# State-space decays: the diagonal blocks get their mask on TensorE, the other blocks go from PSUM straight into their final place

## The reference

```python
def chunked_decay_scan(q, k, v, log_a, s0):
    # S_t = a_t S_{t-1} + k_t^T v_t,  y_t = q_t S_t
    cum = jnp.cumsum(log_a ...)
    decay = jnp.exp(jnp.where(lower, cum[..., :, None] - cum[..., None, :], -jnp.inf))
    scores = jnp.einsum('bhnid,bhnjd->bhnij', qc, kc) * decay
    y_intra = jnp.einsum('bhnij,bhnjv->bhniv', scores, vc)
    ...

def bidir_prefix_scan(ctx_in, lat_in):
    yc_f, sc_f = chunked_decay_scan(context, forward, from zero)
    yc_b, sc_b = chunked_decay_scan(flipped context, backward, from zero)
    yl_f, _ = chunked_decay_scan(latent, forward, from sc_f)
    yl_b, _ = chunked_decay_scan(flipped latent, backward, from sc_b)
```

## Time and profile before

| what | value |
|---|---|
| time of three executions, median (lowest to highest) | 1506.96 us (1502.47 to 1507.47) |
| span of the profiled execution, first to last instruction | 1503.5 us (its time around the span isn't given) |
| mean granted clock of PE | 0.971 of 2.4 GHz |
| PE, DVE, ACT, POOL busy | 1422.7, 818.4, 666.7, 835.4 us |
| first `spread` to start of `out1` | 640.16 to 702.66 us |

### The profile page before, as it was taken

The page is one execution under the profiler, slowest core; times in us unless marked ns, Lnnn a source line. Parts: engine busy times, 40 slices in busy tenths (PEclk is TensorE's granted clock), DMA queues, the critical chain, the costliest instruction groups (busy, mean ns, idle before and its releaser), DMA issues.

```text
span 1503.5 us, 22602 instructions
## 1 busy us (share of the span) xinstructions
PE 1422.7 (95%) x8800; PEld 1215.9 (81%) x8800; DVE 818.4 (54%) x1554; ACT 666.7 (44%) x1076; POOL 835.4 (56%) x665
## 2 busy tenths in 40 slices
PE   6989999999999999877999999999999999999997
PEld 3868888999988887544778888888878865999997
DVE  3787677786676697677675333321126667322211
ACT  3436764445452233674442322232226376544442
POOL 0533417998965443664435454554446630699985
PEclk9999999999999999977999999999999999999999
DMA  9656605777775642000445555543333320355563
GB/s 368 258 181 254 231 18 208 254 251 245 241 254 201 216 161 96 15 29 1 143 151 195 196 185 195 187 140 90 103 104 108 112 89 1 114 195 185 182 188 119
DMA packets 71322, 242.98 MB, mean 162 GB/s; under 512 B 7472, under 2 KB 13104, under 8 KB 70832
## 3 DMA queue, kind: packets, MB, share of 16 engines
q1 hardware_dynamic: 68800, 237.15, 46.5%
q10 hardware_dynamic: 2416, 4.39, 1.0%
HBM read 239.42 MB, written 1.05 MB: 160 GB/s over the span
## 4 chain that ended last, share of the span: by engine, by line
PE 51%; DVE 3%; ACT 2%; POOL 1%; issue 1%; DMA 0%; DVEq 0%; ACTq 0%
PE bank L539 15%; PE bank L540 14%; PE bank L541 14%; PE cond_a L960 1%; PE bank L960 1%; PE bank L676 1%; PE cond_a L1020 1%; PE bank L677 1%; PE bank L968 1%; PE bank L680 1%; PE bank L980 1%; PE cond_b L980 0%; PE cond_b L968 0%; ACT w_hi L1278 0%; DVE scratch L2572 0%
## 5 line engine op out<-in xcount | busy, mean ns | idle before, releaser
L1783 POOL TENSOR_TENSOR w_lo<-raw,w_hi 128x512 fp32r<-128x512 f32 (+1 forms) x612 | 774.0, 1291 | 629.9 <-ACT w_hi L1278 618.0
L1278 ACT ACTIVATE w_hi<-raw 128x1024 fp32r<-128x1024 f32 (+3 forms) x301 | 308.9, 1029 | 601.3 <-PE bank L541 522.5
L539 PE MATMUL bank<-h_hi,w_hi 128*128 128x256 f32 (+2 forms) x1604 | 525.6, 328 | 5.6 <-DVE h_lo L1842 2.6
L541 PE MATMUL bank<-h_hi,w_lo 128*128 128x256 f32 (+2 forms) x1604 | 522.3, 326 | 0.0
L540 PE MATMUL bank<-h_lo,w_hi 128*128 128x256 f32 (+2 forms) x1604 | 522.1, 326 | 0.0
L539 PEld LDWEIGHTS bank<-h_hi,w_hi 128*128 128x128 f32 (+1 forms) x1604 | 302.5, 189 | 38.1 <-DVE h_lo L1842 5.8
L541 PEld LDWEIGHTS bank<-h_hi,w_lo 128*128 128x128 f32 (+1 forms) x1604 | 302.3, 188 | 26.3
L540 PEld LDWEIGHTS bank<-h_lo,w_hi 128*128 128x128 f32 (+1 forms) x1604 | 302.6, 189 | 25.8
L539 PE MATMUL bank<-hidden_hi,w_hi 128*128 128x256 f32 (+1 forms) x528 | 167.6, 317 | 0.5 <-POOL w_lo L1783 0.5
L540 PE MATMUL bank<-hidden_lo,w_hi 128*128 128x256 f32 (+1 forms) x528 | 167.3, 317 | 0.0
L541 PE MATMUL bank<-hidden_hi,w_lo 128*128 128x256 f32 (+1 forms) x528 | 167.3, 317 | 0.0
(11 more groups left out here) (420 smaller groups left out, 1790.7 us busy)
## 6 DMA issues: line engine op xcount, KB each, us to landing
raw<-in_up SPq DMA_DIRECT2D x132, 512.0 KB, 3.5
ada_w<-in_ada SPq DMA_DIRECT2D x128, 512.0 KB, 4.5
raw<-in_down SPq DMA_DIRECT2D x48, 448.0 KB, 3.4
raw<-in_out SPq DMA_DIRECT2D x24, 512.0 KB, 3.5
raw<-in_down SPq DMA_DIRECT2D x24, 512.0 KB, 3.6
raw<-in_in SPq DMA_DIRECT2D x24, 512.0 KB, 3.6
arena<-in_ada SPq DMA_DIRECT2D x16, 512.0 KB, 11.8
raw<-in_uq SPq DMA_DIRECT2D x12, 384.0 KB, 3.0
```

The costliest lines, as they stand in the source:

```text
L539: pe.matmul(out, w_h, x_h, start=first, stop=False)
L541: return pe.matmul(out, w_l, x_h, start=False, stop=last)
L1278: act.activation(part_slot(w_hi, f, u), raw_slot(f, u), ACT.Copy).then_inc(s["rounded"], 1)
L1783: pool.tensor_tensor(part_slot(w_lo, f, u)[:, a:b], raw_slot(f, u)[:, a:b], part_slot(w_hi, f, u)[:, a:b].bitcast(F32), ALU.subtract).then ...
```

## The change

The mask isn't added on DVE any more. `decay_arguments` is gone. For every decay ACT first reads the unmasked bank and writes the blocks that need no mask (`apart`), in their final place: a block between different tiles of tokens is wholly allowed in one direction and wholly masked in the other, so it is written into `ea` by the one direction that has it, and POOL needs not add it. Then PE overwrites the bank (`mask`): it makes the spread again and adds, with an identity as the weights, a 128x128 triangle (`ahead` or `behind`) to all four 128-column blocks. ACT takes the four diagonal blocks from it (`near`). POOL adds only the diagonal blocks (two additions of 256 columns) and the latent columns of the context sources (one of 512). All sixteen calls of `decay_arguments` go (four of them are shown); `apart(q)` has their waits, and waits for `rt_p` before the first and `rt_y` before the third. The identity and the triangles are copied into fp32r by three ACT copies ahead of the retention decays. One buffer of squares moves. PE's, ACT's and DVE's orders are rewritten; the waits for buffers move from DVE to ACT.

```diff
-         "after": after, "before": np.where(s > t, 0.0, NEG),
+         "ahead": np.where(upto, 0.0, NEG), "behind": np.where(upto, NEG, 0.0),
...
+        exact_ident, ahead, behind = (work_r[:, 2, i * P:(i + 1) * P] for i in range(3))
...
-        sq_r = [sq_sum[:, :], work[:, 2, :], sq_2, scratch[:, 0:512]]
+        sq_r = [sq_sum[:, :], sq_1, sq_2, scratch[:, 0:512]]
...
+        def triangle(e, i):
+            return e[:, i, i * P:(i + 1) * P] if i < 2 else e[:, 2, 3 * (i - 2) * P:(3 * (i - 2) + 1) * P]
+
+        def triangles(e, lat):
+            blocks = e.rearrange("p a (b c) -> p (a b) c", c=P)
+            return blocks[:, 8:12:3, :] if lat else blocks[:, 0:6:5, :]
...
                     for i in range(TT):
+                        if between and i == 2:
+                            between()
...
+                def mask(q):
+                    pe.wait_ge(s["sd_apart"], q + 1)
+                    h, d = divmod(q, 2)
+                    pe.matmul(decay_bank(q), picks[0:40, h:h + 1].to_broadcast([40, P]), grow[0:40, d, :],
+                              start=True, stop=False)
+                    pe.matmul(decay_bank(q).rearrange("p (i t) -> p i t", i=TT), exact_ident,
+                              (behind if d else ahead).unsqueeze(1).to_broadcast([P, TT, P]),
+                              start=False, stop=True).then_inc(s["sd_masked"], 1)
...
                     ret_weighted(p)
+                mask(0)
                 ssd_scores(0)
                 pe.wait_ge(s["rt_y"], 4)
                 spread(2)
+                mask(1)
                 pe.wait_ge(s["gn_in"], 4)
...
                 last.then_inc(s["gn_sum"], 1)
+                mask(2)
                 spread(3)
                 spread(4)
-                spread(5)
                 pe.wait_ge(s["gn_inv"], 1)
                 group_spread(0)
                 group_spread(1)
+                mask(3)
+                spread(5)
+                mask(4)
+                group_spread(2)
                 spread(6)
-                group_spread(2)
-                spread(7)
+                mask(5)
                 group_spread(3)
-                spread(8)
-                spread(9)
-                spread(10)
+                for q in (7, 8, 9):
+                    spread(q)
+                    mask(q - 1)
                 pe.wait_ge(s["gn_done"], 4)
-                ssd_weighted(0)
-                spread(11)
-                spread(12)
+                def ahead_of(q):
+                    spread(q)
+                    mask(q - 1)
+                ssd_weighted(0, lambda: ahead_of(10))
+                ahead_of(11)
+                ahead_of(12)
                 ssd_scores(1)
-                spread(13)
-                ssd_weighted(1)
-                spread(14)
-                spread(15)
+                ahead_of(13)
+                ssd_weighted(1, lambda: ahead_of(14))
+                ahead_of(15)
+                mask(15)
                 ssd_weighted(2)
...
+            act.wait_ge(s["tables_in"], 32)
+            for out, table in ((exact_ident, ident), (ahead, C1("ahead")), (behind, C1("behind"))):
+                act.activation(out, table, ACT.Copy)
             for h in range(RH):
                 ret_decays(h)
...
-            def ssd_decays(q):
+            def decays(q, pieces):
+                for out, i, t0, t1_ in pieces:
+                    last = act.activation(out, decay_bank(q)[:, t0:t1_], ACT.Exp, bias=ngs[:, q % 2, i, q // 2:q // 2 + 1])
+                return last
+
+            def apart(q):
+                h, d = divmod(q, 2)
+                total, e = ea[h % 5], eb[h % 2]
...
+                act.wait_ge(s["sd_b"], q + 1)
+                decays(q, ((total[:, 0, P:TOK], 0, P, TOK), (total[:, 1, L0:L1], 1, L0, L1),
+                           (total[:, 2, P:2 * P], 2, L0 + P, L1)) if d == 0 else
+                          ((e[:, 0, L0:L1], 0, L0, L1), (total[:, 1, 0:P], 1, 0, P), (e[:, 1, L0:L1], 1, L0, L1),
+                           (total[:, 2, 2 * P:3 * P], 3, L0, L0 + P))).then_inc(s["sd_apart"], 1)
+
+            def near(q):
+                h, d = divmod(q, 2)
+                e = eb[h % 2] if d else ea[h % 5]
+                act.wait_ge(s["sd_masked"], q + 1)
+                decays(q, [(triangle(e, i), i, i * P, (i + 1) * P) for i in range(TT)]).then_inc(s["sd_e"], 1)
+
+            apart(0)
+            apart(1)
+            near(0)
+            apart(2)
+            near(1)
+            near(2)
             act.wait_ge(s["gn_sum"], 1)
...
+            apart(3)
             for q in range(3, 2 * RH):
-                ssd_decays(q)
+                if q + 1 < 2 * RH:
+                    apart(q + 1)
+                near(q)
                 if 8 <= q < 12:
                     round_y(q - 8)
...
                 pool.wait_ge(s["sd_e"], 2 * h + 2)
-                for i in range(3):
-                    last = pool.tensor_tensor(ea[h % 5][:, i, :], ea[h % 5][:, i, :], eb[h % 2][:, i, :], ALU.add)
+                for lat in range(2):
+                    blocks = triangles(ea[h % 5], lat)
+                    pool.tensor_tensor(blocks, blocks, triangles(eb[h % 2], lat), ALU.add)
+                far = ea[h % 5][:, 0:2, L0:L1]
+                last = pool.tensor_tensor(far, far, eb[h % 2][:, 0:2, L0:L1], ALU.add)
                 last.then_inc(s["sd_sum"], 1)
...
-                decay_arguments(0)
                 keep_ret(3)
-                decay_arguments(1)
-                decay_arguments(2)
-                decay_arguments(3)
...
-                ssd_weigh(0)
                 dve.wait_ge(s["gn_std"], 1)
                 dve.reciprocal(gn_inv, gn_inv).then_inc(s["gn_inv"], 1)
+                ssd_weigh(0)
```

More of the change, by code:

```diff
@@ L305, in build @@
         dt, log_r, nega, decay_tmp = c(TT, 16), c(16), c(16), c(16)
+        sq_1 = c(512)
         swap_r = y1[:, 0:4, :].rearrange("p a (b t) -> p (a b) t", b=2)
@@ L360, in build @@
             "swap_done", "log_ready", "rt_sum", "sd_sum", "rt_s", "rt_e", "rt_p", "rt_o", "rt_y",
-            "gn_mid", "gn_inv", "gn_in", "gn_sum", "gn_spread", "gn_std", "gn_act", "gn_done", "dt_cols", "dt_ready", "dt_log", "gn_gate", "sd_t", "sd_tt", "sd_b", "sd_s",
-            "sd_arg", "sd_e", "sd_p", "sd_o", "sd_y", "sn_in", "sn_sq", "sn_acc", "sn_sum", "sn_std", "sn_inv", "sn_spread",
+            "gn_inv", "gn_in", "gn_sum", "gn_spread", "gn_std", "gn_act", "gn_done", "dt_cols", "dt_ready", "dt_log", "gn_gate", "sd_t", "sd_tt", "sd_b", "sd_s",
+            "sd_apart", "sd_masked", "sd_e", "sd_p", "sd_o", "sd_y", "sn_in", "sn_sq", "sn_acc", "sn_sum", "sn_std", "sn_inv", "sn_spread",
             "lk_sq", "lk_in", "lk_sum", "lk_std", "lk_inv", "lk_spread", "lk_work", "lk_hi", "lk_done",
@@ L1009, in ret_scores, with weighted @@
                         last.then_inc(s["rt_s"], 1)
-                def weighted(p, v, taken, out, done, probs):
+                def weighted(p, v, taken, out, done, probs, between=None):
                     if p >= 2:
@@ L1027, in ret_weighted, with ssd_weighted @@
                     weighted(p, vr, s["rt_y"], 6, s["rt_o"], ra)
-                def ssd_weighted(p):
+                def ssd_weighted(p, between=None):
                     pe.wait_ge(s["sd_p"], 6 * p + 6)
-                    weighted(p, xt, s["sd_y"], 5, s["sd_o"], ea)
+                    weighted(p, xt, s["sd_y"], 5, s["sd_o"], ea, between)
                 def spread(q):
@@ L1656, in _ @@
             round_next()
-            def ssd_decays(q):
-                h, d = divmod(q, 2)
[L1661 to L1670, removed]
@@ L1672, in _ @@
-            for q in range(3):
-                ssd_decays(q)
+            def decays(q, pieces):
[3 more added lines that the diff above has]
+            def apart(q):
+                h, d = divmod(q, 2)
+                total, e = ea[h % 5], eb[h % 2]
+                if q == 0:
+                    act.wait_ge(s["rt_p"], 12)
+                if q == 2:
+                    act.wait_ge(s["rt_y"], 4)
+                if d and h >= 2:
+                    act.wait_ge(s["sd_sum"], h - 1)
+                if not d and h == 3:
+                    act.wait_ge(s["gn_gate"], 1)
+                if not d and h == 4:
+                    act.wait_ge(s["gn_gate"], 4)
+                if not d and h >= 5:
+                    act.wait_ge(s["sd_o"], (h - 5) // 2 + 1)
+                act.wait_ge(s["sd_b"], q + 1)
[3 more added lines that the diff above has]
+                           (total[:, 2, 2 * P:3 * P], 3, L0, L0 + P))).then_inc(s["sd_apart"], 1)
@@ L2524, in keep_ret @@
                     dve.tensor_tensor(sq_r[p], y1[:, p, :], y1[:, p, :], ALU.mult).then_inc(s["gn_in"], 1)
-                def decay_arguments(q):
-                    h, d = divmod(q, 2)
-                    e = eb[h % 2] if d else ea[h % 5]
-                    if d and h >= 2:
-                        dve.wait_ge(s["sd_sum"], h - 1)
-                    if not d and h == 3:
```

(13 more changed lines are left out.)

12 lines of the change are left out of this document (removed).

## The result

The changed kernel takes 1514.47 us (median of 6 runs, 1513.51 to 1516.61). The kernel before, run beside it, takes 1504.7 us (6 runs, 1500.8 to 1507.47). The ratio is 1.0066, with a 95% interval of 1.0048 to 1.0085: slower by 9.8 us, where 5.1 were forecast. The direction and its reason were right; one price was too low. The forecast time, 1512.1 us, is only 2.4 us off, and that is in part luck: it was built on a time before of 1506.96 us (three runs), 2.3 above the 1504.7 of the six runs, and this took away half of the error of 4.7 us in the difference. The difference itself, +9.8, lies outside the forecast's own range of +1.5 to +9.

A forecast was written before the change was run, and what follows sets the result against it. No engine is full; the order of four in-order queues decides. Copies +0.7 and the last weighting's later start +4.4 make +5.1 us, added to 1506.96: 1512.1 us, range 1501 to 1518 (forecast's own range +1.5 to +9).

The forecast's parts named there:

- DVE's additions leave the chain, masks take their place: Between 640 and 703 us: DVE's mask additions, 6.2 us on the chain of waits, go; PE gets 16 masks.
- The mask's price: On PE: two 512-column matmuls, each 0.23 us at full clock, twice that at half: a mask is 0.46 or 0.92.
- To the group norm: After the last retention weighting: first group spread at 657.0 instead of 656.40 us; ACT starts decay 3 2.4 us later.
- Weighting 0: PE's weighting 0 starts +2.5 us later, behind mask(8); at its end, for which apart(10) waits, the delay is +3.6.
- To weighting 1: From weighting 0's end: exponents, scores, spread and masks take 9.3 us (8.3 to 10.7), before 6.9; sum +6.0.
- The tail: From weighting 1 on: longer arm through weighting 2, its gate and the last product; last weighting starts +4.4 us.
- ACT's and POOL's prices: ACT exponents step 0.36 us for 256 columns, 0.26 for 128; POOL's sum takes 2.7 us a head, before 3.7.
- Full clock (1): PE's clock stays full and the masks vanish in gaps: -4.5 us with the copies, 1502.5 us; chance 0.15.
- DVE the holder (2): The 6.2 us of DVE mask additions leave the chain and nothing takes their place: 1501.5 us; chance 0.13.
- Half clock throughout (3): PE at half clock through the weightings: +10.8 us with the copies, 1517.8 us; chance 0.08.
- Dear short exponents (4): On ACT a 128-wide exponent costs as much as a 256-wide, 0.8 us more a decay: +4, 1516 us; chance 0.09.
- No trace of it (5): The change doesn't show, queues re-pack within 1 us: 1507 us; chance 0.05.

The follow-up runs named there:

- product_first: The changed kernel with head 7's product ahead of the gate of weighting 2 on DVE: 1517.16 us, 1.0071 of the kernel before.
- mask_signal: The changed kernel with each mask's two matmuls left out, all waits kept, diagonal blocks taken without exponential: 1504.04 us, 0.9986 of the kernel before.
- diagonal_on_dve: The kernel before with DVE masking only diagonal blocks, ACT placing unmasked blocks finally, POOL's sums shrunk, no masks on PE: 1502.12 us, 0.9970 of before.

## Why the prediction was right in sign and short in size

- **DVE's additions leave the chain, masks take their place.** Right; DVE lost 19.8 us in the stage (47.9 to 28.1), the chain shows masks instead, and without their matmuls the loss is gone.
- **The mask's price, the step that failed.** The prediction took "0.46 or 0.92" us from `out1`'s 0.23 a matmul. Measured: 0.65 and 1.44. The ten masks of the chain have 10.2 us, where the forecast's prices give 7 x 0.46 + 3 x 0.92 = 6.0: 4.2 short. With them the last weighting would start at +8.6 instead of +4.4, and +9.5 was measured. (That the whole came to +9.8 isn't accounted for so closely: the last weighting gave 0.9 back, and what lies ahead of the stage is not resolved.) The step of back-to-back matmuls in a linear layer wasn't the nearest row for a matmul that comes alone, with weights of its own; it lacked a fixed part of 0.09 to 0.29 us. The trace of before held a nearer one, a lone `spread` at the half clock, 0.72 us from its start to the next (668.42):

```profile
667.70 0.79 PE L1038 MATMUL cond_b<-work_r,picks 40*128 40x512 f32 x1 [2.28 <-ACT arena L1669]
```

The prediction's own sign of this error, a mask of over 1 us, came true at half clock.
- **To the group norm.** The first group spread came 18.46 us behind the first `spread`; 16.24 before, 16.8 forecast. The masks up to it explain most; the half means also took 4.4 us instead of the 3.66 assumed.
- **Weighting 0.** Measured from the first `spread`, it starts 5.0 us later than before (33.33 against 28.33), forecast +2.5; its end +5.6, forecast +3.6. That apart(10) must wait for this end was right: ACT idles 2.8 us there, releaser PE L1032, in the waits above, and 2.2 us ahead of apart(14), where the prediction had 3 or more for each.
- **To weighting 1.** 10.25 us from the end of weighting 0, forecast 9.3, before 6.9: within its bounds of 8.3 to 10.7 (its own terms, 4.4, 2.8 and 0.7, make the lower one 7.9). The sum stood at +8.95, forecast +6.0.
- **The tail.** The last weighting starts +9.5 (66.66 us behind the first `spread`, before 57.18), forecast +4.4; the interval is 66.7, forecast 61 to 62. The arm by way of the gate was the right one, as product_first shows. The last weighting itself took 4.48 instead of 5.39 us.
- **ACT's and POOL's prices.** Right. ACT's timeline of after, group by group, has 256 and 128 columns 0.36 and 0.25 apart (forecast 0.36 and 0.26), and POOL's a sum of 2.6 us (forecast 2.7):

```profile
668.05 0.49 ACT L1697 ACTIVATE arena<-cond_a,spare 128x256 f32<-128x256 f32 x1
668.41 0.39 ACT L1697 ACTIVATE scratch<-cond_a,spare 128x128 f32<-128x128 f32 x1
668.66 0.51 ACT L1697 ACTIVATE arena<-cond_a,spare 128x256 f32<-128x256 f32 x1
```

```profile
672.67 1.41 POOL L1884 TENSOR_TENSOR scratch<-scratch,arena 128x256 f32<-128x256 f32 x2 [1.77 <-ACT arena L1697]
674.04 1.27 POOL L1886 TENSOR_TENSOR scratch<-scratch,arena 128x512 f32<-128x512 f32 x1
```

- **The rivals.** Full clock (1): the stage had 0.78 (and its sum 680.2 + 3.4 + 11.0 is 694.6, not 694.8). DVE the holder (2): without the masks' matmuls it was, in part, for mask_signal and diagonal_on_dve run at 1504.0 and 1502.1, where the rival had 1501.5; with them PE is. Half clock throughout (3): no, 0.73 to 0.92 in the stretches up to weighting 2; its size, +10.8, is the nearest to the +9.8 measured, but that came by way of the mask's price. Dear short exponents (4): no, 0.25 us. No trace of it (5): no.

## What to carry to other kernels

Price an inserted matmul from a row where it stands as it will, alone and with weights of its own, at both clock levels; a linear layer's spacing, with each load ahead of its matmul, shows the cheapest case. When a change has two halves, here cheaper placing and another engine for the mask, cost and try them apart: one half gained 0.3% and the other lost three times as much. A round trip between two queues is priced by what stands behind the waiting instruction: about nothing through PE here, 8 to 11 us through DVE in the order tried.

## What was not expected of the hardware

- With its weight load recorded together with it, a spread of 512 columns took 0.42 us at the full and 0.72 us at the half level, beside 0.23 us a matmul in `out1` at the full one: a fixed part of 0.21 and 0.29 us. The Trainium skill (TensorE: Matmul & The Clock Gate, Architectural detail) says that loads are pulled ahead of matmuls in flight. In `out1` the trace agrees (0.22 us ahead), and so it does at a mask's spread right behind another one (0.23 us); at none of the sixteen identity matmuls does it, and why is open.
- Less work did not mean less time on PE: with 128 instead of 512 columns in 32 matmuls, the stage's mean clock went from 0.78 to 0.66 and PE's busy time from 59.6 to only 58.8 us.
- The single identity matmul (128 rows) and the single spread (40 rows), both of 512 columns, in the same places, came with mean clocks of 0.84 and 0.67. ACT's exponents were shorter in the first, so the matmul alone isn't shown to be the reason.
- On ACT, an exponent of 128 columns out of PSUM followed the one before after 0.26 us with a bias and after 0.16 without.
